# Sample states loaded twice and sample outputs moved ahead of the scores in a hybrid conv/HGRN2/MoE layer

## The reference, cut to what matters

```
proj = rmsnorm(x) @ w_in                  # cv cg q f v og ga gb
u = cv * sigmoid(cg); c = silu(layernorm(depthwise_conv31(u))); y_a = c @ w_conv_out
fg = lb + (1-lb)*sigmoid(f); k = 1-fg
S_t = diag(fg_t) S_(t-1) + k_t v_t^T;  o_t = S_t^T q_t          # per head
y_b = (rmsnorm(o) * silu(og)) @ w_hgrn_out
m = sigmoid(ga)*y_a + sigmoid(gb)*y_b;  x += m @ w_out
```

## Time and profile before

| | |
|---|---|
| time, median of 3 runs | 871.23 us (869.25 to 871.9) |
| the profiled execution's own time | 869.31 us |
| its span, first to last instruction | 867.5 us |
| mean granted TensorE clock | 0.984 of full |
| PE busy | 807.5 us (93%) |
| VectorE, ScalarE, POOL busy | 256.7, 152.5, 107.6 us |
| HBM read, written | 255.07 MB, 12.09 MB |

### The profile page before, as it was taken

One profiled execution on the slowest core, in us unless ns is written; L12 is line 12 of the kernel. 1 busy time (PEld: TensorE's weight loads), 2 busy tenths in 40 slices (PEclk: granted clock), 3 DMA queues, 4 the chain that ended last, 5 costly groups with the idle time before them and its releaser, 6 DMA issues.

```text
span 867.5 us, 9404 instructions
## 1 busy us (share of the span) xinstructions
PE 807.5 (93%) x3845; PEld 469.2 (54%) x3845; DVE 256.7 (30%) x541; ACT 152.5 (18%) x238; POOL 107.6 (12%) x127
## 2 busy tenths in 40 slices
PE   6999989968699999999999999999899889989996
PEld 4888868857688888886333333333232323323332
DVE  3069995363255221234110011100110111011103
ACT  4014312223401250014111110010000100010002
POOL 4100052233333000003000000000300000000001
PEclk9999989989999999999999999999999999999999
DMA  8855322436856967239999999999999999999992
GB/s 306 263 176 207 109 97 98 128 82 185 202 146 208 410 266 286 102 122 322 430 427 416 408 428 425 428 426 427 429 425 428 426 428 425 426 430 419 422 422 119
DMA packets 68148, 267.34 MB, mean 308 GB/s; under 512 B 5510, under 2 KB 31186, under 8 KB 52735
## 3 DMA queue, kind: packets, MB, share of 16 engines
q1 hardware_dynamic: 66346, 263.46, 77.7%
q0 software_dynamic: 640, 2.16, 0.7%
q10 hardware_dynamic: 1117, 1.08, 0.4%
HBM read 255.07 MB, written 12.09 MB: 308 GB/s over the span
## 4 chain that ended last, share of the span: by engine, by line
PE 63%; DMA 23%; SPq 6%; DVE 5%; issue 1%; ACT 1%; POOL 1%; ACTq 0%; DVEq 0%; POOLq 0%
PE bank L1732 17%; PE bank L1408 16%; DMA slots<-in_w_expert_gate_dram 14%; PE bank L1770 8%; PE bank L1642 7%; DMA gb<-in_state_hgrn_dram 4%; PE bank L1779 4%; DMA slot<-in_w_expert_gate_dram 4%; SPq L481 3%; DVE gb L1001 2%; PE bank L1589 2%; SPq L429 2%; DVE slot L985 1%; PE bank L1422 1%; SPq L445 1%
## 5 line engine op out<-in xcount | busy, mean ns | idle before, releaser
L1408 PE MATMUL bank<-hT,slots 128*128 128x264 f32 x896 | 212.3, 397 | 0.7 <-DVE hT L940 0.7
L1732 PE MATMUL bank<-slots,hT 128*64 128x512 f32 x688 | 193.5, 595 | 9.3 <-DMA slots<-in_w_expert_gate_dram 9.3
L1408 PEld LDWEIGHTS bank<-hT,slots 128*128 128x128 f32 x896 | 173.7, 197 | 31.5 <-issue 1.7
L1278 DVE TENSOR_TENSOR early<-early,bank 128x512 f32<-128x512 f32 x16 | 11.0, 688 | 391.4 <-PE bank L1732 391.4
L1732 PEld LDWEIGHTS bank<-slots,hT 128*64 128x64 f32 x688 | 59.6, 137 | 110.1 <-issue 94.5
L1770 PE MATMUL bank<-slots,wrep 128*64 128x512 f32 x336 | 106.4, 595 | 5.4 <-ACT wrep L858 5.4
L1732 PE MATMUL bank<-slot,hT 128*64 128x512 f32 x256 | 76.3, 594 | 3.2 <-DMA slot<-in_w_expert_gate_dram 3.2
L685 POOL COPY hT<-early 128x512 f32 x30 | 17.6, 615 | 385.9 <-PE bank L1732 291.1
L1779 PE MATMUL bank<-hT,diag 128*128 128x512 f32 x128 | 59.2, 605 | 0.0
L1770 PEld LDWEIGHTS bank<-slots,wrep 128*64 128x64 f32 x336 | 32.2, 137 | 47.9 <-issue 40.3
L985 DVE SCALAR_TENSOR_TENSOR slot<-slot,rows_buf 128x256 f32<-128x256 f32 x120 | 55.7, 539 | 0.0
(11 more groups left out here) (272 smaller groups left out, 760.4 us busy)
## 6 DMA issues: line engine op xcount, KB each, us to landing
slots<-in_w_expert_down_dram SPq DMA_DIRECT2D x19, 2048.0 KB, 30.5
slots<-in_w_expert_up_dram SPq DMA_DIRECT2D x18, 2048.0 KB, 30.7
slots<-in_w_expert_gate_dram SPq DMA_DIRECT2D x18, 2048.0 KB, 30.7
slots<-in_w_in_dram SPq DMA_DIRECT2D x14, 2048.0 KB, 10.0
slot<-in_w_expert_gate_dram SPq DMA_DIRECT2D x8, 2048.0 KB, 27.9
slot<-in_w_expert_up_dram SPq DMA_DIRECT2D x5, 2048.0 KB, 28.6
slot<-in_w_expert_down_dram SPq DMA_DIRECT2D x5, 2048.0 KB, 33.1
slots<-in_w_expert_gate_dram SPq DMA_DIRECT2D x8, 1024.0 KB, 22.1
```

The lines of the kernel that those rows point to most:

```text
L1408: last = mm(out, w[:, a, t * P:(t + 1) * P], hT[:, a, :], start=(a == 0), stop=(a == KT - 1))
L1732: last = mm(out[sl, :], xe[:, a, sl], expert_view(p, kind, e, a // 4)[:, a % 4, :], start=(a == 0), stop=(a == KT - 1))
```

## The change

- The old states of each pair are loaded twice. First all four pairs for o_rows, alternately into `gb` and `ga` (OLD_IN), at load 0, 7 and 8 of the weight stream. Then again for the new states (NEW_IN): pairs 0 and 1 at load 9, pair 2 at load 11 behind the store of pair 1 and the values of pair 3, pair 3 at load 12 behind the store of pair 2.
- On PE, all o_rows and o_samples move into chunks 6 and 7, the mean after chunk 7, the variance after tile (8,1), the turned values 4, 5 before it, 0 to 3 into chunk 9. The own product (`dqk`) stands behind o_rows(0). It is now added in two steps on VectorE once v is there.
- VectorE takes 4, 4 and 8 taps where it took 8, 8 and the rest, with the copies of the samples' outputs between. `states_add` waits for the new state load, not for o_rows; states_add(4) and (6) stand ahead of the level 4 and late level 5 copies.
- Pairs 0 and 2 of the values have a tile of their own in slot7 (where the convolution's input and then its squares lie) and come in one DMA with 1 KB rows. Pairs 1 and 3 are loaded as before. The loads wait for the variance.
- POOL's order becomes 0 1 2 3 s0 s1 s2 s3 4 s4 s5 5 s6 s7 6 7 8.
- The mean squares use eight banks: four of `proj`, two of `scores`, two of `misc`.

```diff
-        S0 = gb[:, :, :].rearrange("p a t -> p (a t)")[:, 0:2 * D].rearrange("p (r b d) -> p r b d", r=2, b=NB)
+        S0 = [x[:, :, :].rearrange("p a t -> p (a t)")[:, 0:2 * D].rearrange("p (r b d) -> p r b d", r=2, b=NB) for x in (gb, ga)]
+        OLD_IN = {0: (0, 1), 1: (1, 1), 2: (0, 2), 3: (1, 2)}
+        NEW_IN = {0: (0, 3), 1: (1, 3), 2: (0, 4), 3: (0, 5)}
+        STORED = {0: (0, 1), 1: (1, 1), 2: (0, 2), 3: (0, 3)}
...
+            def load_values(p):
+                if p % 2:
+                    for h in (2 * p, 2 * p + 1):
+                        sp.dma_start(vrep(h), v_rows[:, h * P:(h + 1) * P].partition_broadcast(P)).then_inc(v_in[1], 16)
+                else:
+                    sp.dma_start(slot7[:, KT * T:KT * T + 2 * D].rearrange("p (b n) -> p b n", b=NB),
+                                 v_rows[:, 2 * p * P:(2 * p + 2) * P].partition_broadcast(P)).then_inc(v_in[0], 16)
...
             for c in range(STREAM, HO + 1):
                 load(c)
+                if c == 7:
+                    sp.wait_ge(conv_stored, 32)
+                    load_states(1, OLD_IN[1])
+                if c == 8:
+                    for p in (2, 3):
+                        sp.wait_ge(misc.ready, misc.written(("os", 2 * p - 4)))
+                        load_states(p, OLD_IN[p])
+                if c == 9:
+                    for p in (0, 1):
+                        sp.wait_ge(misc.ready, misc.written(("os", 2 * p + 4)))
+                        load_states(p, NEW_IN[p])
                 if c == 10:
                     sp.wait_ge(*misc.read(("vt", 5)))
                     sp.dma_start(v_rows[:, :], vrow).then_inc(v_stored, 16)
                     sp.wait_ge(v_stored, 16)
+                    sp.wait_ge(proj.ready, proj.written("var"))
                     load_values(0)
                     load_values(1)
...
+                if c == 11:
+                    store_states(0)
+                    load_values(2)
+                    store_states(1)
+                    load_values(3)
+                    wait_stored(0)
+                    load_states(2, NEW_IN[2])
+                if c == 12:
+                    store_states(2)
+                    wait_stored(2)
+                    load_states(3, NEW_IN[3])
+                if c == 13:
+                    store_states(3)
...
-            for work in (0, 1, 2, 3, "s0", "s1", 4, "s2", "s3", 5, "s4", "s5", 6, 7, "s6", "s7", 8):
+            for work in (0, 1, 2, 3, "s0", "s1", "s2", "s3", 4, "s4", "s5", 5, "s6", "s7", 6, 7, 8):
```

More of the change, by code:

```diff
@@ L994, in states_add @@
             def states_add(h0):
-                dve.wait_ge(misc.ready, misc.written(("os", h0)))
+                home, count = NEW_IN[h0 // 2]
+                dve.wait_ge(state_in[home], 32 * count)
                 for h in (h0, h0 + 1):
@@ L1144, in _ @@
                 dve.tensor_copy(score[:, 4 * i:4 * i + 4, P:SEQ], src[:, :].rearrange("p (a c) -> p a c", a=4)).then_inc(S_dve, 1)
-            o_rows(6)
             dve.wait_ge(*proj.read(("ga", KT - 1)))
-            gated_a(0)
-            gated_a(1)
-            states_add(6)
-            gated_a(2)
-            gated_a(3)
+            for d in range(4):
+                gated_a(d)
             turned_keys(0)
-            o_samples(6)
             gated_a(4)
@@ L1453, in o_rows @@
                 pe.wait_ge(own_ready, 2)
-                for h in (h0, h0 + 1):
-                    pe.wait_ge(state_in[h % 2], 16 * (h // 2 + 1))
+                home, count = OLD_IN[h0 // 2]
+                pe.wait_ge(state_in[home], 32 * count)
                 misc.before_write(pe, ("os", h0))
@@ L1461, in o_rows @@
                         end = SEQ + 4 * g + j + 1
-                        last = mm(out[32 * j:32 * j + 32, i * P:(i + 1) * P], q[:, h, end - 32:end], S0[:, h % 2, 4 * g + j, :],
+                        last = mm(out[32 * j:32 * j + 32, i * P:(i + 1) * P], q[:, h, end - 32:end], S0[home][:, h % 2, 4 * g + j, :],
                                   start=True, stop=True, tile_position=(0, 32 * j))
@@ L1506, in _ @@
             in_projection(5)
-            for t in range(4):
-                in_tile(6, t)
-                if t == 0:
-                    pe.wait_ge(k_ready, HEADS)
-                diagonal(t)
+            in_tile(6, 0)
+            o_rows(0)
+            own_products()
+            in_tile(6, 1)
+            pe.wait_ge(k_ready, HEADS)
+            diagonal(0)
+            o_samples(0)
+            in_tile(6, 2)
+            diagonal(1)
+            o_rows(2)
+            in_tile(6, 3)
+            diagonal(2)
+            o_samples(2)
             def turned_values(i):
@@ L1520, in _ @@
             in_tile(7, 0)
+            diagonal(3)
+            o_rows(4)
+            in_tile(7, 1)
             level(0, (0, 1))
-            in_tile(7, 1)
+            o_samples(4)
+            in_tile(7, 2)
+            level(0, (2, 3))
+            o_rows(6)
+            in_tile(7, 3)
+            level(1, (0, 1))
+            o_samples(6)
             pe.wait_ge(conv_ready, 1)
```

201 lines of the change are left out of this document (103 added, 98 removed).

## The result

The kernel after takes **877.24 us** (median of 7 runs, 873.98 to 879.62) against 871.23 for the kernel before: ratio 1.0065, 95% interval [1.0042, 1.0088], some 5.7 us slower. A ratio compares the means of the executions, so it can differ a little from that of the medians. The forecast was 875.6, slower, with a range of 864.5 to 883. The profiled execution took 874.24 us (span 872.4, mean granted clock 0.976); before it was 869.31 (867.5, 0.984). HBM read rose from 255.07 to 259.26 MB, the 4 MB of states read twice.

The account below looks back on a forecast made before the run. Expert weights bound the second part, tied to the hand-over; TensorE's holes cost 31.0 us before it. New waits and half clock 34.4 against 31.0, POOL +1.9, squares -0.9: +4.4 on 871.2 gives 875.6 us, range 864.5 to 883.

Parts of the forecast that it names:

- The waits of part 1: TensorE's new waits at the early outputs: 1.4 us at o_rows(0) for own_ready, 4.1 at o_samples(0) for VectorE's copy.
- 1 KB rows: Load of pair 0's values in 1 KB rows: transfer taken as 7.5 us, between 4 and 10.4.
- The rival by which pair 0 comes no quicker than before: 1 KB rows no quicker than 512-byte ones: pair 1 lands 2.9 us later, +7.3, 878.5 us; chance 0.10.
- Pair 1's values: Landing at 190.7 us, behind pair 0; TensorE then waits 5.7 us at level 3's second half.
- the first rival: Values of pairs 0 and 1 land within 14 us, break-even about 188: -5.8, 865.4 us, faster; chance 0.28.
- the collision: POOL's work on pair 2's values blocks VectorE's states_add(2): 0 to 8.5 us, taken as one instruction, 1.9.
- The level 4 wait: TensorE waits 14.9 us for level 4 copies, which stand behind states_add(4) and pair 2's reloaded states in VectorE's order.
- the rival with the full collision: All four POOL instructions hold VectorE's state update: 8.5 us instead of 1.9, +11, 882 us; chance 0.12.
- Half clock: TensorE at 1.2 GHz behind its longer new waits: 3.1, 2.6 and 2.6 us, together 8.3.
- The first part in sum: Before the hand-over to the experts: 34.4 us of new waits and half clock against 31.0 removed; +4.4 with POOL and squares.
- the squares: Mean squares in eight banks: TensorE's 0.7 us wait for ScalarE's read goes, with its restart: -0.9 us.
- The second part moves one for one with the hand-over: The expert part, bound by weight loads, passes each microsecond won or lost ahead of it to the end.

Follow-up runs that it names:

- experiment 7: Kernel after with the values of pairs 0 and 2 in 512-byte rows, two DMAs instead of one: 872.2 us, ratio 1.0029.
- experiment 3: Kernel after with states_add(4) behind the first level 5 copies and states_add(6) between the gated tiles in VectorE's order: 869.41 us, ratio 0.9976.
- experiment 5: Kernel after with one wait added: POOL starts sample head s4 only after VectorE's states_add(2) is done: 869.86 us, ratio 0.9979.
- experiment 9: Kernel after with SyncE's load of the row table held back until POOL has issued its fourth scatter: 874.57 us, ratio 1.0008.
- experiment 4: Kernel after with POOL's decayed_qk(4) ahead of sample heads s2 and s3: 869.18 us, ratio 0.997.
- experiment 8: Kernel after with SyncE's load of the row table held back until POOL has issued its sixth scatter: 876.05 us, ratio 1.0041.
- experiment 10: Kernel before with POOL's six scatters held until the first store of the quad table has landed: 876.62 us, ratio 1.0047.

## Why the prediction was right, and where it was not

- **The waits of part 1** (forecast 1.4 and 4.1): 1.25 and 4.0. The three waits for old states and the late add are gone, as forecast.
- **1 KB rows** (7.5 us of transfer, between 4 and 10.4): right. Landing 9.3 us after issue against 9.1, and 12.0 with 512-byte rows in experiment 7. The rival by which pair 0 comes no quicker than before falls, and so does the one by which values come within 14 us: pair 1 landed 16.9 after the first issue. The Trainium skill, "DMA: Bandwidth & Descriptors", "Specifications", has 512 B as the least transfer for full rate; experiment 7 (12.0 against 9.3) speaks against it for these reads of v_rows.
- **Pair 1's values** (190.7; wait 5.7): mis-sized. They landed at 187.4, 7.6 us behind pair 0 where the 10.4 of the kernel before were taken over; the wait was 3.0. In five other executions with this order they came 7.9 to 9.8 us behind it. In experiment 7, too, pair 0 took the 12.0 us of the kernel before, and pair 1 only some 9.3 more. The landing lay past the break-even of 188 that the first rival names, and yet the kernel is slower: the rival let the collision go with it, and the collision grew. Why the second pair in a queue is quicker no run tells.
- **The level 4 wait** (14.9, with one collision of 1.9): right in mechanism, as experiments 3 and 5 show. It was 18.25, of which experiment 5 gives 5.2 to the collision, so 13.0 without it, against the 14.9 forecast: the loads took 20.4 us where 21.6 was taken, and TensorE's own work meanwhile 18.2 instead of 16.9. The collision was mis-sized, at 1.9 where it cost 5.6: three of POOL's instructions lay over the update, since pair 2's values landed 7 us sooner than forecast, and the blocked work was the whole of one half update. So the rival with the full collision (chance 0.12) came near the truth, at two thirds of its 8.5. That VectorE and POOL block each other is what the Trainium skill, "SBUF — State Buffer", "Who interferes with whom", says; this trace agrees for VectorE (7.83 against 2.18), while POOL's own instructions beside it hardly grew (2.41 against 2.35).
- **Half clock** (8.3): 6.6. The prediction lets each longer wait bring it. At 3 us that is not certain: behind a wait of 3.03 us in experiment 9 and of 2.98 in experiment 4 the same score group took 2.02 us, at the full granted clock, and behind 3.03 us in the kernel after 3.75.
- **The first part in sum** (+4.4): new waits 26.5 and half clock 6.6 make 33.1, less 31.0 and less 0.9 for the squares: +1.2. POOL's power operation starts 1.7 later in the profiled execution. The same instruction varies by some microseconds between executions of the same first part (391.5 to 395.2 in four with it, 389.9 to 390.5 in three with the one before); their means differ by 3.0.
- **The second part moves one for one with the hand-over**: this step failed, and the prediction had named it as a sign of being wrong. The tail grew by 3.2 to 3.9 us, from the order of 1.5 MB of loads and six scatters in the DMA queues, a microsecond apart. Experiments 8 to 10 show the late landing in both directions; that it makes the tail longer rests on single profiled executions, which agree with each other. No term of the forecast stood for it. So 875.6 came that near to 877.2 partly by luck: a first part taken too dear (4.4 against 1.7 to 3.0) made up for a tail taken at nothing.

What stays open: why SyncE's store of the quad table lands about a microsecond sooner in the kernel after (2.3 us from the second store's issue to the row table's, against 3.3 and 3.5 in the kernel before and 3.0 with 512-byte rows), which is what moves the row table ahead; from that store to the sixth scatter it is 4.8 us in all of these. No run tells it.

## What to carry to other kernels

When a wait for a DMA leaves the bottleneck engine, look for the instruction that now waits in its place, and ask what stands behind it in its engine's order: here the same reload, 18 us late, sat in front of the copies that free TensorE's banks, and moving it behind them, with POOL kept off the updates and two of its steps moved ahead, turned a loss of 0.6% into a gain of 1.8%. Move an instruction only with a look at what it will run beside: the move alone gained a third of that, since the moved update took 13.0 us instead of 4.3. And compare the distance from a late landmark to the end as well as the landmark: a part that the edit doesn't touch can change by the order in which queues are filled.

## What the runs showed of the hardware that was not expected

- Reads of a small DRAM tensor spread to all partitions do not go by bytes alone: 1 MB took 9.3 us from issue to use as one DMA in 1 KB rows and 12.0 as two in 512-byte rows.
- Eight VectorE updates of 2.2 us took 6.4 to 9.2 beside POOL, and sixteen of 4.3 took 11.4 to 13.0. A POOL instruction that waits for VectorE cost nothing and took 5.2 us off TensorE's longest wait.
- Six indirect scatters landed 3.0 us after the last issue where the loads were held back until the sixth was issued, and 13.1 us with 1.5 MB of loads issued 2.4 us ahead of it; at 1.3 us ahead, TensorE's rows were there in time. A 0.5 MB fetch took 3.5 us in the kernel after, issued when the DMA engines stood idle, and 12.4 with 3.5 MB of loads issued in the 1.9 us ahead of it.
- After waits of some 3 us TensorE went on at 1.2 GHz in some executions and at 2.4 in others: 3.75 and 2.02 us for the same 16 matmuls.
